# Attention output by features: the values as the stationary operand on two halves of the array, the softmax division before the product, the gate by features

## What is computed

```python
# first block, layers 0 and 1: 8 heads of 64 features, 2 key/value heads, window 128
p = jnp.exp(s - m)
p = p / (jnp.sum(p, axis=-1, keepdims=True) + jnp.exp(sink - m))
o = jnp.einsum('bhgnqk,bnkhd->bnqhgd', p, vb)
a = sliding_window_attention(q, k, v, attn_sinks[layer]) * jax.nn.silu(z_attn)
merged = (jax.nn.sigmoid(gate_attn) * (a @ w_up_attn[layer])
          + jax.nn.sigmoid(gate_hgrn) * (b @ w_up_hgrn[layer]))
# second block: 8 heads with a value head each, causal, no gate z
probs = jax.nn.softmax(logits, axis=-1)
y_att = einsum('bhqk,bhkd->bhqd', probs, vh)
merged = jax.nn.sigmoid(ga) * (y_att @ w_out_att[i]) + ...
```

## Time and profile before

| | us |
|---|---|
| median of 3 runs | 815.09 |
| lowest and highest run | 814.96, 815.3 |
| the profiled execution's own time | 814.28 |
| its span in the profile | 812.6 |
| TensorE matmul busy | 796.2 |
| VectorE busy | 597.4 |
| ScalarE busy | 476.7 |

### The profile page before, as it was taken

The page is one execution under the profiler, slowest core; times in us unless marked ns, Lnnn a source line. Parts: engine busy times, 40 slices in busy tenths (PEclk is TensorE's granted clock), DMA queues, the critical chain, the costliest instruction groups (busy, mean ns, idle before and its releaser), DMA issues.

```text
span 812.6 us, 12834 instructions
## 1 busy us (share of the span) xinstructions
PE 796.2 (98%) x5184; PEld 720.3 (89%) x5184; DVE 597.4 (74%) x690; ACT 476.7 (59%) x562; POOL 28.0 (3%) x63
## 2 busy tenths in 40 slices
PE   8999999999999999999999999999988999999998
PEld 8988899998998889999887999999877888888877
DVE  7799775668578787576667667556779877786883
ACT  6775775442776596543457644543468656565682
POOL 8100000000000000300000000000000000000000
PEclk9999999999999999999999999999999999999999
DMA  8545443454435633255736434464139979797921
GB/s 274 191 155 183 136 153 105 155 197 169 154 111 201 206 106 105 104 197 173 246 104 207 156 105 156 156 208 156 52 104 364 324 265 343 256 333 262 340 101 52
DMA packets 70043, 149.65 MB, mean 184 GB/s; under 512 B 8458, under 2 KB 11104, under 8 KB 69984
## 3 DMA queue, kind: packets, MB, share of 16 engines
q1 hardware_dynamic: 69568, 148.78, 52.6%
q0 software_dynamic: 384, 0.04, 0.1%
q10 hardware_dynamic: 32, 0.01, 0.0%
HBM read 147.76 MB, written 1.05 MB: 183 GB/s over the span
## 4 chain that ended last, share of the span: by engine, by line
PE 86%; DVE 8%; ACT 2%; DMA 2%; issue 1%; SPq 1%; POOL 0%; DVEq 0%; POOLq 0%; ACTq 0%
PE mm L616 11%; PE mm L618 11%; PE mm L617 11%; PE mm L600 9%; PE mm L602 9%; PE mm L601 9%; PE aux L1080 4%; PE aux L1078 4%; PE aux L1079 4%; DVE sb_w_lo L1637 3%; PE aux L708 3%; PE aux L803 3%; PE aux L766 1%; DVE sb_gb L1637 1%; PE aux L743 1%
## 5 line engine op out<-in xcount | busy, mean ns | idle before, releaser
L1637 DVE TENSOR_TENSOR sb_w_lo<-sb_raw,sb_w_hi 128x2048 fp32r<-128x2048 f32 (+2 forms) x153 | 318.7, 2095 | 58.1 <-ACT sb_w_hi L1486 27.0
L1192 ACT ACTIVATE sb_w_hi<-sb_raw 128x2048 fp32r<-128x2048 f32 (+1 forms) x83 | 155.1, 1871 | 151.1 <-PE mm L618 113.5
L616 PE MATMUL mm<-sb_hT_hi,sb_w_hi 128*128 128x256 f32 x592 | 170.1, 287 | 0.0
L618 PE MATMUL mm<-sb_hT_hi,sb_w_lo 128*128 128x256 f32 x592 | 167.4, 283 | 0.0
L617 PE MATMUL mm<-sb_hT_lo,sb_w_hi 128*128 128x256 f32 x592 | 167.4, 283 | 0.0
L1486 ACT ACTIVATE sb_w_hi<-sb_raw 128x2048 fp32r<-128x2048 f32 x50 | 95.9, 1917 | 38.3 <-PE aux L1080 16.7
L600 PE MATMUL mm<-sb_w_hi,sb_hT_hi 128*128 128x512 f32 (+1 forms) x296 | 112.1, 379 | 4.1 <-DVE sb_w_lo L1637 4.1
L616 PEld LDWEIGHTS mm<-sb_hT_hi,sb_w_hi 128*128 128x128 f32 x592 | 113.4, 192 | 1.4 <-issue 1.3
L617 PEld LDWEIGHTS mm<-sb_hT_lo,sb_w_hi 128*128 128x128 f32 x592 | 113.5, 192 | 0.0
L618 PEld LDWEIGHTS mm<-sb_hT_hi,sb_w_lo 128*128 128x128 f32 x592 | 113.4, 191 | 0.0
L602 PE MATMUL mm<-sb_w_hi,sb_hT_lo 128*128 128x512 f32 (+1 forms) x296 | 110.2, 372 | 0.0
(11 more groups left out here) (400 smaller groups left out, 1341.3 us busy)
## 6 DMA issues: line engine op xcount, KB each, us to landing
sb_raw<-in_w_in SPq DMA_DIRECT2D x120, 512.0 KB, 4.4
sb_raw<-in_w_down SPq DMA_DIRECT2D x32, 512.0 KB, 5.5
sb_raw<-in_w_gate SPq DMA_DIRECT2D x31, 512.0 KB, 4.8
sb_raw<-in_w_up SPq DMA_DIRECT2D x31, 512.0 KB, 6.3
sb_raw<-in_w_out SPq DMA_DIRECT2D x16, 512.0 KB, 4.4
sb_raw<-in_w_up_attn SPq DMA_DIRECT2D x8, 512.0 KB, 4.1
sb_raw<-in_w_up_hgrn SPq DMA_DIRECT2D x8, 512.0 KB, 4.2
sb_raw<-in_w_o SPq DMA_DIRECT2D x8, 512.0 KB, 4.4
```

The costliest lines, as they stand in the source:

```text
L616: pe.matmul(dst, w[0][:, k, cs], acts[0][:, k, :], start=start, stop=False, skip_group_check=True)
L618: return pe.matmul(dst, w[1][:, k, cs], acts[0][:, k, :], start=False, stop=stop, skip_group_check=True)
L1192: act.activation(w_hi[:, slot(t), 0:width], raw[:, slot(t), 0:width], ACT.Copy).then_inc(hi_split, 1)
L1637: return dve.tensor_tensor(out_, a, b, op)
```

## The change

The probabilities are divided by their sum before they are transposed (`softmax_norm`, one VectorE instruction over 128 x 1024 per unit, new semaphore `p_normed`). In `pv` the values stand (64 columns) and the probabilities move; even heads write partitions 0 to 63 of the result and odd heads 64 to 127, so that the result has features on its partitions. For unit 0 of the first block two heads with the same values share one matmul of 256 columns. The job AT and its transposes go. z is made by `group_T`, scaled out of PSUM by VectorE (`by_feature_out`, new semaphore `z_scaled`) and put through Silu by ScalarE in place (`z_silu`). In the first block VectorE multiplies the result with z straight into `a_T` (the buffer of `a_tok`); in the second ScalarE and VectorE split it unit by unit (`unit_high`, `unit_rest`).

```diff
 def p_transposes(turn, u, n):
-    pe.wait_ge(S["p_ready"], n * 3 + (u + 1))
+    pe.wait_ge(S["p_normed"], n * 3 + (u + 1))
     transposes(turn, [s_ring[:, u % 2, i * P:(i + 1) * P] for i in range(8)])
-def pv(turn, u, n, vpart):
+def pv(turn, u, n, vpart, shared):
     pe.wait_ge(S["pT_ready"], n * 3 + (u + 1))
     ps = begin(turn)
-    if u == 0:
-        for h in range(8):
-            last = pe.matmul(ps[:, h * 64:h * 64 + 64], pT[:, h * P:(h + 1) * P], vpart(h, 0), start=True, stop=True)
+    p_of = pT[:, :].rearrange("p (m q) -> p m q", q=P)
+    if u == 0 and shared:
+        for kv in range(2):
+            for odd in range(2):
+                last = pe.matmul(ps[64 * odd:64 * odd + 64, 2 * kv * P:2 * (kv + 1) * P], vpart(4 * kv, 0),
+                                 p_of[:, 4 * kv:4 * kv + 4, :].rearrange("p (c o) q -> p c o q", o=2)[:, :, odd, :],
+                                 start=True, stop=True, skip_group_check=True)
+    elif u == 0:
+        for h in range(8):
+            last = pe.matmul(ps[64 * (h % 2):64 * (h % 2) + 64, h // 2 * P:(h // 2 + 1) * P], vpart(h, 0),
+                             p_of[:, h, :], start=True, stop=True, skip_group_check=True)
     else:
-        for i in range(4):
+        for c in range(2):
             for kt in range(2):
-                last = pe.matmul(ps[:, i * 64:i * 64 + 64], pT[:, (2 * i + kt) * P:(2 * i + kt + 1) * P],
-                                 vpart(unit_heads(u)[i], kt), start=kt == 0, stop=kt == 1)
+                for odd in range(2):
+                    i = 2 * c + odd
+                    last = pe.matmul(ps[64 * odd:64 * odd + 64, c * P:(c + 1) * P], vpart(unit_heads(u)[i], kt),
+                                     p_of[:, 2 * i + kt, :], start=kt == 0, stop=kt == 1, skip_group_check=True)
...
-                         18: [lambda: pvs(2)], 19: [b_transposes], 20: [a_transposes],
+                         18: [lambda: pvs(2)], 19: [b_transposes],
...
-                    form = group_T if name in ("fh", "qh", "ga0", "ga1", "gb0", "gb1") else group
+                    form = group_T if name in ("fh", "qh", "z", "ga0", "ga1", "gb0", "gb1") else group
...
+                def z_silu():
+                    act.wait_ge(S["z_scaled"], L + 1)
+                    act.activation(z[:, :, :], z[:, :, :], ACT.Silu).then_inc(S["z_ready"], 1)
...
-                    12: [lambda: mm_out("z", z, S["z_ready"], ACT.Silu), lambda: level_exp(6)],
+                    12: [lambda: level_exp(6), z_silu],
...
-            def softmax_out(u, n, turn, sinks, gate):
+            def softmax_norm(u, n, sinks):
...
                 link(dve.reciprocal(ast[:, 0, a:a + nh], ast[:, 2, a:a + nh]))
...
+                p = s_ring[:, u % 2, :].rearrange("p (h k) -> p h k", h=nh)
+                tt_(p, p, ast[:, 0, a:a + nh].unsqueeze(2).broadcast_to([P, nh, 1024 // nh]), ALU.mult
+                    ).then_inc(S["p_normed"], 1)
...
-                    12: [lambda: unit_in(0), lambda: levels(6)], 13: [wait_z, lambda: unit_in(1)],
-                    14: [lambda: levels(7)],
+                    12: [lambda: unit_in(0), lambda: levels(6), lambda: by_feature_out("z", z_flat, S["z_scaled"])],
+                    13: [lambda: unit_in(1), lambda: unit_norm(0)],
+                    14: [lambda: levels(7), wait_z, lambda: unit_norm(1)],
...
                     16: [lambda: take_level(7), lambda: level_factors(8),
-                         lambda: by_feature_out("ga0", by_feature(ga, 0), S["gate_in"])],
+                         lambda: by_feature_out("ga0", by_feature(ga, 0), S["gate_in"]), lambda: unit_norm(2)],
...
-                7: [lambda: unit_in(0)], 8: [lambda: unit_in(1), lambda: by_feature_out("cc", E[1])],
-                10: [lambda: unit_out(0), lambda: unit_in(2), make_u],
-                11: [conv], 12: [lambda: unit_out(1)], 13: [conv_gate],
+                7: [lambda: unit_in(0)], 8: [lambda: unit_in(1), lambda: unit_norm(0), lambda: by_feature_out("cc", E[1])],
+                9: [lambda: unit_norm(1)],
+                10: [lambda: unit_rest(0), lambda: unit_in(2), make_u],
+                11: [conv, lambda: unit_norm(2)], 12: [lambda: unit_rest(1)], 13: [conv_gate],
```

More of the change, by code:

```diff
@@ L194, in build @@
         gb = sb("gb", [P, KT, TT * P])
[L195 removed]
+        z = sb("z", [P, 4, TT * P])
         g = sb("g", [P, TT, W])
@@ L287, in build, with unit_of, unit_psum @@
         fw = gb_flat[:, 0:D]
+        z_flat = z[:, :, :].rearrange("p c t -> p (c t)")
+        def unit_of(t, u):
+            if u == 0:
+                return t[:, :, 0:P]
+            return t.rearrange("p (g j) t -> p g j t", j=2)[:, :, u - 1, P:2 * P]
+        def unit_psum(bank, u):
+            n = 4 if u == 0 else 2
+            return bank[:, 0:n * P].rearrange("p (c t) -> p c t", c=n)
         diag = rt[:, 0:2].rearrange("p a t h e -> p (a t h e)")[:, 0:TT * P].rearrange("p (t n) -> p t n", t=TT)
@@ L838, in pvs @@
                         pe.wait_ge(S["v_ready"], L + 1)
-                    pv(job(f"V{u}"), u, L, lambda h, kt: v_sb[:, kt, 64 * (h // 4):64 * (h // 4) + 64])
+                    pv(job(f"V{u}"), u, L, lambda h, kt: v_sb[:, kt, 64 * (h // 4):64 * (h // 4) + 64], True)
                 def b_transposes():
@@ L931, in pvs2 @@
                     pe.wait_ge(S["vh_ready"], 3)
[L932 to L936, removed]
+                pv(job(f"V{u}"), u, 2, lambda h, kt: vh[:, kt, h * 64:h * 64 + 64], False)
             def p2_transposes():
@@ L1352, in a_split @@
                 def a_split():
[L1353 to L1356, removed]
+                    act.wait_ge(S["a_ready"], L + 1)
+                    act.activation(aT_hi[:, :, :], a_T, ACT.Copy).then_inc(S["aT_hi_ready"], 1)
+                def z_silu():
+                    act.wait_ge(S["z_scaled"], L + 1)
+                    act.activation(z[:, :, :], z[:, :, :], ACT.Silu).then_inc(S["z_ready"], 1)
                 def T_out(dst, name, width, event, **kw):
@@ L1453, in split_out, with unit_high @@
                 act.activation(dst, aux[pair][:, 0:width], ACT.Copy).then_inc(event, 1)
+            def unit_high(u):
+                pair, value = AUX2.turn(f"V{u}")
+                act.wait_ge(aux_ready[pair], value)
+                act.activation(unit_of(aT_hi, u), unit_psum(aux[pair], u), ACT.Copy).then_inc(S["aT_hi_ready"], 1)
             def y_split():
@@ L2053, in unit_in, with unit_norm @@
                     softmax_in(u, L, AUX1.turn(f"S{u}", L), sinks)
+                def unit_norm(u):
+                    softmax_norm(u, L, sinks)
                 def unit_out(u):
-                    softmax_out(u, L, AUX1.turn(f"V{u}", L), sinks, z)
+                    pair, value = AUX1.turn(f"V{u}", L)
+                    dve.wait_ge(aux_ready[pair], value)
+                    ins = tt_(unit_of(a_T, u), unit_psum(aux[pair], u), unit_of(z, u), ALU.mult)
+                    release(ins, aux_free[pair], value)
+                    if u == 2:
+                        dve.sem_inc(S["a_ready"], 1)
                 def next_gain():
@@ L2206, in unit_in, with unit_norm, unit_rest @@
                 softmax_in(u, 2, AUX2.turn(f"S{u}"), None)
-            def unit_out(u):
-                softmax_out(u, 2, AUX2.turn(f"V{u}"), None, None)
+            def unit_norm(u):
+                softmax_norm(u, 2, None)
+            def unit_rest(u):
+                pair, value = AUX2.turn(f"V{u}")
+                dve.wait_ge(S["aT_hi_ready"], 3 + u)
+                ins = tt_(unit_of(aT_lo, u), unit_psum(aux[pair], u), unit_of(aT_hi, u).bitcast(F32), ALU.subtract)
+                release(ins, aux_free[pair], value, S["aT_lo_ready"])
             def merged(name, gate, c, other=None):
```

54 lines of the change are left out of this document (16 added, 38 removed).

## The result

| | before | after |
|---|---|---|
| median (lowest, highest) of 5 runs, us | 815.09 (814.5, 815.3) | 818.58 (818.38, 820.73) |
| ratio, 95% interval | | 1.0048, 1.0034 to 1.0063 |
| profiled execution, us | 814.28 | 818.59 |
| its span, us | 812.6 | 816.8 |
| mean granted clock of TensorE | 1.00 | 0.995 |

The change costs 3.5 us. In all five runs of the changed kernel TensorE's mean granted clock is 0.994 to 0.996, so the profiled one is typical of them. First the page of the changed kernel: busy times and granted clock.

What follows compares the result with a forecast made beforehand. TensorE, busy 796.2 of 812.6 us, was taken as the bound. Terms -2.6 + 1.0 - 4.3 + 7.6 = +1.7 us on the profiled 814.28, with the median 0.8 above, gave 816.8 us; 8-in-10 range 814.4 to 823.5.

Steps and rivals of the forecast that it cites:

- the mechanism itself: Forecast's own case, both wait and product terms right: 815.3 to 818.3 us, chance 0.62.
- transposes of the output: TensorE's 8 transposes of the attention output go in each of three stages, 0.88 us each: -2.6 us.
- z by features: Two z tiles in each of two layers take 5.83 us as `group_T` instead of 5.58: +1.0 us.
- products: Nine product units on divided columns take 1.26 to 1.29 us instead of 1.73 to 1.83: -4.3 us.
- new wait: TensorE waits 3.8 us for VectorE's division before unit 0's transposes in layers 0 and 1: +7.6 us.
- clock: Rival: TensorE's clock falls after standing still, tile 14 at half speed; +3 to +11 us, 820 to 828, chance 0.04.
- the chain is held by z: In layers 0 and 1, z's Silu and a table load on ScalarE delay unit 0's exponentials: wait 3.8 us.
- the rival: Chain not held by z: exponentials not pushed back, TensorE waits 1.5 us, 812.2 us, faster; chance 0.12.
- TensorE would stand still 3.8 us twice: Stands before unit 0's transposes in layers 0 and 1; a clock fall could add up to 5.8 us per layer.
- The other end of the bound, 1.91: Product unit length in us if column halves do not overlap: products +1.3 instead of -4.3, 822.4 us; chance 0.22.
- Overlap of the halves: Products of even and odd heads on separate column halves run beside each other, as in the scores; underlies the -4.3 us.
- Costed at nothing: VectorE's added divisions and z scaling, 1.22 us each, cost nothing because VectorE is idle a quarter of the span.

Runs made afterwards that it cites:

- run 4: Changed kernel with 14 filler matmuls on TensorE ahead of the wait in layers 0 and 1, their result overwritten: 815.34 us, ratio 1.0006 to the kernel before.
- run 1: Changed kernel with ScalarE's Silu of z moved from step 12 to step 14, beside g's Silu: 811.76 us, ratio 0.9959 to the kernel before.
- run 5: Silu and scaling of z later, level 6 before the transposes, plus all even heads' product matmuls before the odd heads': 811.71 us, against 807.85 without that reordering.
- run 2: Changed kernel with z's Silu later on ScalarE and VectorE's scaling of z moved behind unit 0's division: 809.49 us, ratio 0.9931 to the kernel before.
- Run 6: Kernel before with only the division moved ahead of the transposes; z by tokens, products and output transposes as before: 816.86 us, ratio 1.0025.

## Why the prediction was right and where it was off

The direction and the wide range (814.4 to 823.5) hold: forecast 816.8, slower the likeliest, measured 818.58. The narrow range of the mechanism itself, 815.3 to 818.3, was missed, and one of the prediction's own signs of being wrong came true: the granted clock left full speed behind the wait. The forecast's single steps did unequally well.

| step | predicted us | measured us |
|---|---|---|
| transposes of the output | -2.6 | -2.6 |
| z by features | +1.0 | +1.2 |
| products | -4.3 | -5.6 |
| new wait | +7.6 | +7.2 |
| clock | 0 (rival) | +2.8 |
| sum | +1.7 | +3.0 |

The profiled span rose by 4.2, of which 0.43 lay ahead of the change; 0.8 remain without a row.

**Luck in the direction.** Without the clock the measured steps add up to +0.2, and run 4, which kept the clock up, can't be told from the kernel before (1.0006, 0.9997 to 1.0015). The forecast of +1.7 lies above that mainly because it put the products 1.3 us too dear. That the kernel is clearly slower comes from the clock, which stood at nothing in the sum. Two errors of opposite sign brought the number close.

**The new wait** was right in size, 3.59 and 3.58 against 3.8, and in every link. Its start was forecast 0.5 us later than before for z's two tiles; these took 0.6 a layer. The forecast that the chain is held by z is confirmed by run 1: freed from Silu, the wait was 1.7, where the rival gave 1.5 for just that case. That the times agree as well (811.76 against 812.2) is in part chance, since the rival's sum has the products 1.3 too dear. No wait in the second block, as forecast.

**The step that failed** is "TensorE would stand still 3.8 us twice" with its price of zero in the sum and 0.04 in the chances. The prediction said itself that the trace had no such stand and could not exclude a fall, so nothing it had read supported a chance as small as 0.04. It happened in one of the two layers. Its price there, 2.8 us, is less than the 5.8 named, since the clock was back 0.8 us into tile 14: what ran slowly was mainly transposes and level 6. Run 4 gives 3.2 for it. Had this term stood in the sum once, with 2.8, the forecast would have been 819.6.

**The products** were mis-sized by 1.3 us, on the safe side. A unit took 1.02, and 1.14 with the changes into and out of the divided array, not 1.29. The changes cost 0.12 and not 0.20: the tile before a product takes 5.92, not 5.83, and about 0.03 more falls behind it. The other 0.07 is the difference between the scores' 1.09 and 1.02. The picture behind the number, a pass of one head beside a pass of the next, does not fit the runs either: the scores, too, move 2048 columns in a unit, and their 1.06 to 1.09 us lie near the 0.96 that as many columns take in the tiles (run 5). The other end of the bound, 1.91, was not a bound: with the halves in turn, which is the case that it meant, the run shows 1.51. Its pace of 0.107 was read from rows that all have 128 columns standing, and was taken for the price of an instruction whatever its shape.

**Overlap of the halves.** Run 5 shows 1.51 us in turn and 1.02 alternated for the same 16 instructions on the same rows of the array: what has to be done for one half of the columns can partly be hidden behind the other's. The Trainium skill, TensorE: Matmul & The Clock Gate, Part 3 (Packing small matmuls), lets loads overlap only where the row group differs. By it alternation would have gained nothing. The measurement decides against it here.

**Costed at nothing.** VectorE's added work did cost nothing while ScalarE was last, and run 2 priced it once it was not: 2.3 us for both layers' scaling. So it cost nothing in this order only. Run 6, with the division alone, came out 1.8 us slower than the kernel before; 0.8 of that is its wait, and the rest stayed open.

## What to carry to other kernels

When a change puts a second engine between two steps of the engine that bounds, follow the whole in-order queue of that engine: here a Silu that was made by 95.6 and first read at 114.58 (VectorE's product with z) stood ahead of the exponentials. Moving it alone gave back 6.8 us (818.6 to 811.8), nearly all of the 7.0 that the change saved in TensorE's own work; moving VectorE's scaling and level 6 as well led to 807.9. A new stand of some microseconds on TensorE is to be priced also with the work behind it at half clock, with a real chance: it happened in one of two here. In these fp32 products with 64 or 128 moving columns, fewer standing columns and alternating halves of the array both made a unit shorter, so it paid to let the small operand stand. With 256 moving columns the order of the halves made no difference.

## What the runs showed of the hardware that was not expected

- In two stands of 3.59 and 3.58 us, with TensorE busy before each, the granted clock stayed at full speed in one and fell to half in the other, from 303.2 to 310.0. What made the difference was not found.
- 16 fp32 instructions take 1.79 us with 128 columns standing, 1.51 with 64 in turn and 1.02 with 64 alternated; their weight loads last 192 and 136 ns.
- Where the halves alternate, sharing one matmul between two heads is worth nothing: 8 instructions of 256 moving columns take 1.01 us (unit 0 of the first block) and 16 of 128 take 1.02 (483.06 to 484.08 in the second block). One half after the other, it is worth 0.49 us: 1.02 against 1.51 (run 5).
